# Two weight copies moved ahead of a sigmoid, and three convolution taps moved behind the last states

## The reference, cut to what matters

```python
# one layer, fp32; x (1, 1024, 1024), ctx (1, 256, 1024), d_ff = 2816
px = split_proj(modulate(x, ...) @ w_in)     # q, f_fwd, f_bwd, v, g, conv a, conv b
s = sigmoid(pre); f = lb + (1 - lb) * s; k = (1 - lb) * (1 - s)
# group A, 4 heads, two directions: S_t = diag(f_t) S_{t-1} + k_t v_t^T, o_t = S_t^T q_t
y = rms_norm_per_head(o) * onorm_g * silu(p_g)
# group B, 512 channels: u = p_a * sigmoid(p_b); depthwise convolution of width 31 along
# rows of 64 tokens; + bias; LayerNorm over the channels; silu
x = x + gate1 * rms_norm(concat(A, B) @ w_out)
x = x + gate2 * rms_norm((silu(h @ wg) * (h @ wu)) @ wd)     # h = modulate(x, ...)
```

## Time and profile before

| | us |
|---|---|
| median of 3 runs (lowest, highest) | 1451.61 (1450.51, 1451.93) |
| profiled execution, its own time | 1452.88 |
| its span, first to last instruction | 1451.1 |
| TensorE busy in the span | 1375.9 |
| VectorE, ScalarE, GpSimd busy | 778.6, 377.3, 324.2 |

### The profile page before, as it was taken

How to read it: one execution, slowest core, us unless ns; L and a number is a source line. 1 busy time by engine, 2 the same in 40 slices (tenths; PEclk the granted TensorE clock), 3 DMA queues, 4 the chain that set the end, 5 groups by cost and what they waited for, 6 DMA issues and landing times. The chain is left out here.

```text
span 1451.1 us, 17647 instructions
## 1 busy us (share of the span) xinstructions
PE 1375.9 (95%) x6725; PEld 1148.5 (79%) x6725; DVE 778.6 (54%) x1020; ACT 377.3 (26%) x562; POOL 324.2 (22%) x135
## 2 busy tenths in 40 slices
PE   6699899999999997898989999999999999999998
PEld 1588788888888886687768888888888888888876
DVE  2899969769778879818721313232232313232227
ACT  3521222132232234616631121111111121111112
POOL 1522111021111124503524122122122122122110
PEclk9699799999999998999999999999999999999999
DMA  9384110110010010004321111101101111101132
GB/s 370 155 284 165 29 30 16 30 44 28 29 43 29 14 68 34 1 25 164 136 68 29 50 39 58 58 31 57 57 29 58 49 39 57 58 30 57 51 124 116
DMA packets 94704, 101.94 MB, mean 70 GB/s; under 512 B 3118, under 2 KB 77091, under 8 KB 94658
## 3 DMA queue, kind: packets, MB, share of 16 engines
q1 hardware_dynamic: 94658, 101.32, 20.5%
HBM read 92.92 MB, written 8.39 MB: 70 GB/s over the span
## 5 line engine op out<-in xcount | busy, mean ns | idle before, releaser
L1238 POOL TENSOR_TENSOR slot<-slotraw,slot 128x1024 fp32r<-128x1024 f32 x66 | 160.5, 2442 | 522.2 <-ACT slot L1174 313.8
L561 PE MATMUL bank<-h2Ta,slot 128*128 128x512 f32 x1056 | 247.5, 394 | 5.2 <-POOL slot L1238 4.9
L561 PE MATMUL bank<-slot,mid 128*128 128x512 f32 x1056 | 242.9, 391 | 1.8 <-POOL slot L1238 1.8
L561 PEld LDWEIGHTS bank<-h2Ta,slot 128*128 128x128 f32 x1056 | 200.4, 190 | 47.8 <-POOL slot L1238 5.3
L561 PEld LDWEIGHTS bank<-slot,mid 128*128 128x128 f32 x1056 | 199.3, 189 | 43.8 <-POOL slot L1238 2.2
L561 PE MATMUL bank<-cathi,slot 128*128 128x512 f32 x704 | 220.2, 389 | 0.0
L1419 DVE SCALAR_TENSOR_TENSOR cat<-conv_u,taps,cat 128x784 f32 (+29 forms) x120 | 150.6, 1255 | 12.6 <-DVE cat L1419 6.2
L561 PEld LDWEIGHTS bank<-cathi,slot 128*128 128x128 f32 x704 | 132.1, 188 | 27.7 <-issue 0.3
L561 PE MATMUL bank<-hT,ringb 128*128 128x512 f32 (+1 forms) x672 | 149.1, 378 | 0.4 <-DVE cat L1402 0.4
L1694 DVE TENSOR_TENSOR mid<-bank,sgm 128x512 f32<-128x512 f32 x44 | 30.4, 692 | 221.7 <-ACT sgm L1189 221.7
L1719 DVE TENSOR_TENSOR arena<-bank,arena 128x512 f32<-128x512 f32 x144 | 99.5, 691 | 90.0 <-PE bank L561 89.5
(11 more groups left out here) (171 smaller groups left out, 1516.7 us busy)
## 6 DMA issues: line engine op xcount, KB each, us to landing
mraw<-in_w_mod SPq DMA_DIRECT2D x48, 512.0 KB, 7.0
slotraw<-in_ffn_w_gate SPq DMA_DIRECT2D x22, 512.0 KB, 3.7
slotraw<-in_ffn_w_up SPq DMA_DIRECT2D x22, 512.0 KB, 3.8
slotraw<-in_ffn_w_down SPq DMA_DIRECT2D x22, 512.0 KB, 3.9
ringinb<-in_w_in SPq DMA_DIRECT2D x12, 512.0 KB, 3.6
xst<-in_x SPq DMA_DIRECT2D x8, 512.0 KB, 13.7
ringina<-in_w_in SPq DMA_DIRECT2D x8, 512.0 KB, 4.7
ringinc<-in_w_in SPq DMA_DIRECT2D x8, 512.0 KB, 4.7
```

The lines of the kernel that those rows point to most:

```text
L561: return pe.matmul(o, l, r, start=start, stop=stop, skip_group_check=True)
L1238: return pool.tensor_tensor(lo, full, hi.bitcast(F32), ALU.subtract)
```

## The change

On ScalarE, the first two weights of round two (slots 0 and 1) are rounded right behind the third sigmoid of round one, ahead of the fourth. The other two stay where they were, behind the copies of positions 2 and 3. On VectorE, in each pass of the head loop, three of the four taps of unit 11 move to unit 12, which has six then instead of three. They stand behind the last states and behind the gated product of unit 12, and ahead of the head's output. Nothing else changes.

```diff
-TAPS_AFTER = [0, 0, 0, 0, 1, 1, 1, 1, 3, 2, 4, 4, 3, 3, 3, 3, 0, 1, 0, 0]
+TAPS_AFTER = [0, 0, 0, 0, 1, 1, 1, 1, 3, 2, 4, 1, 6, 3, 3, 3, 0, 1, 0, 0]
...
                     act.activation(sgm[:, p, :], bank[gu_at(n, pos)[2]][:], ACT.Sigmoid).then_inc(gu_sig, 1)
+                    if first(n) and pos == 2:
+                        gu_hi(1, 0)
+                        gu_hi(1, 1)
...
                     act_pair(n, pair, par)
                     if not last(n):
-                        for j in range(4) if first(n) and pair else range(2 * pair, 2 * pair + (0 if first(n) else 2)):
+                        for j in range(2 * pair, 2 * pair + (2 * pair if first(n) else 2)):
                             gu_hi(n + 1, j)
```

## The result

The changed kernel takes 1441.9 us (median of 4 runs, 1441.65 to 1442.15), the kernel before 1451.77 (4 runs, 1450.51 to 1452.92): a ratio of 0.9935, 95% interval 0.9923 to 0.9947. That is 9.9 us faster; forecast were 9.0 and a time of 1442.6.

What follows compares the result with a forecast made beforehand. TensorE, busy for 95% of the span, was taken as the bound. The terms 4.0 + 2.8 + 5.1 - 2.9 give 9.0 us gained, so 1442.6 us against a median of 1451.61; the range was 1438.8 to 1447.0.

Steps and rivals of the forecast that it cites:

- Idle time at round two: Feed-forward part, start of round two: with early weight copies TensorE restarts at 757.02 instead of 761.06, gaining 4.0 us.
- The clock behind it: The 48 matmuls behind round two's restart run at 2.4 GHz instead of 1.2, gaining 2.8 us.
- The passes: Head loop: TensorE's wait of 1.70 us for the last states goes in each of three passes, gaining 5.1 us.
- The last head: Behind the loop: VectorE, 0.84 late, lets GpSimd ahead of its first Q product; TensorE's level two starts 2.9 us late.
- the first: Rival: the sixth tap precedes GpSimd, so no lag and no loss in the last head; gain 11.9, 1439.7 us; chance 0.20.
- The second: Rival: the last head takes all of the taps' gain; gain 5 to 6.8, 1444.8 to 1446.6 us; chance 0.20.
- the third: Rival: round two's restart waits for something the GpSimd wait hid, only the taps work; gain 2.2, 1449.4 us; chance 0.05.
- the fourth: Rival: six taps behind unit 12 make VectorE the bound of every pass; 3.7 slower, 1455.3 us; chance 0.04.

Runs made afterwards that it cites:

- part A alone: Only the two early weight copies, taps as in the kernel before: 1445.32 us against that kernel's 1451.46, ratio 0.9959.
- part B alone: Only the three taps moved, weight copies as in the kernel before: 1448.01 us, ratio 0.9978 against that kernel.
- warm: The kernel before plus 18 matmuls with unread results in TensorE's wait at the start of round two: 1448.58 us against 1451.47, ratio 0.9979.
- lag: `fit` with the maximum over half of F done twice on VectorE in the last head: 1442.22 us against 1439.95 without it.
- after_again: The changed kernel, unaltered, measured once more on the same chip as `fit`: 1441.55 us, ratio 0.9929 against the kernel before.
- after_third: The changed kernel, unaltered, measured on one chip beside a version rounding only slot 0 early: 1442.93 us; the kernel before took 1451.0 there.
- fit: The changed kernel with two moved taps directly behind the last states, ahead of unit 12's product: 1440.13 us, ratio 0.9918; once more, 1439.95.

## Why the prediction was right

The four terms, forecast and measured in the repeating columns of the table:

- **Idle time at round two:** 4.0, measured 3.94 (part A alone: 56.78 to 52.85). The restart is bound by the fourth product, 0.95 of waiting where 0.85 was expected.
- **The clock behind it:** 2.8, measured 2.8 (690.0 to 687.2; 2.5 by part B alone's 689.7). `warm` shows it apart: 2.9 without any change of the restart.
- **The passes:** 5.1, measured 6.00. This term was too small, by 0.30 in each pass. I took the idle time of the row, 1.70. That idle time counts from the end of the last matmul, which ran from 504.52 to 504.90; such matmuls follow each other after 0.23, so without a wait the next one would have started at 504.75, 0.15 earlier. And the first two matmuls behind the wait took 0.49, where they take 0.38 now, another 0.11. The two are 0.26 of the 0.30; the rest is open. From unit 12's sigmoid to the first square of the output it was 504.94 to 512.27 before, and is 499.67 to 505.03 now, 1.97 less.
- **The last head:** 2.9 back, measured 3.10. The sixth tap is the held one, as forecast (3.10 long, where 3.3 was expected), and GpSimd passes the first Q product. The lag was 1.13 (512.36 against 511.09 + 0.14) and not 0.84, because TensorE gained 2.0 and not 1.7. Once GpSimd is ahead, one block more is paid (VectorE stands through one more subtraction), and the lag's size matters little: some 0.9 in `lag` cost 2.9, 1.13 here 3.1.

The sum is 9.6 against 9.0, and the medians differ by 9.9, by 9.9 again in the second comparison (`after_again`) and by 8.1 in the third (`after_third`). So the mechanism was right in all four terms, but that the time came within 0.7 of the forecast is partly luck. The profiled executions differ by 11.2; the rest of that, 1.3 ahead of the loop, 1.6 at the very end, less 1.3 on the way to round one, came and went in other executions of the same kernels.

Of the rivals, the first is refuted by the stages (the last head did give back; GpSimd's request came 0.73 ahead of the fifth tap's end, at 507.14 against 507.87, where the margin was put at 0.44), though `fit` shows that its 3.1 can be had. The second, a loss of 5, did not occur; the third and the fourth neither: no other wait hid behind GpSimd's, and VectorE's list never held a pass up. What the prediction had only as "some of the clock's uncertainty" is that the placing of low-clock stretches moves one and the same kernel by 1.4 to 1.6 us in a stage (148.93 and 150.54, 685.6 and 687.2), as much as fit gains over the changed kernel.

## What to carry to other kernels

A wait that goes is worth its idle time, plus what a low clock behind it cost, where there was one, less what the freed engines now collide with downstream. Look for the place where two engines hold each other up in turn. Here VectorE came first by only 0.07 us (0.08 in `fit`), and a lag of some 0.9 cost a whole further block of 2.9; how small a lag would do it wasn't tried. When work has to move on an engine, put it into that engine's next idle time and not only behind the wait: the same taps, two of them placed ahead of unit 12's product, gave nothing back in the last head. And compare stages between common points: the medians showed 1.6 for `fit`, and the stages that it was 3.1 gained and, in those profiles, some 2 lost in another place.

## What the runs showed that was not expected

The idle time that the profile gives before a matmul was 0.30 us less than what TensorE lost in each wait for S: three waits of 1.69 to 1.71 in each of three kernels, and passes of 295.89 to 295.93 against 289.91 to 289.94. And 4.24 us of matmuls whose result nothing reads, put into a wait of 4.9, made the kernel 2.9 us faster: the granted clock behind them was 1.00 and not 0.50.
